# Conditioning of a two-block transformer kernel in 48 groups of one 2 MB load instead of 24 of two, spread evenly over the first mixer

## What is computed

```python
def ada_params(cvec, w, b):
    return jnp.split(jax.nn.silu(cvec) @ w + b, 6, axis=-1)   # w: 1024 x 6144
```

## Time and profile before

| what | value |
|---|---|
| median of three executions | 3366.84 us |
| the profiled execution's own time | 3363.03 us |
| its span, first to last instruction | 3361.3 us |
| mean granted TensorE clock | 0.903 |
| TensorE busy | 2707.1 us, 81% of the span |
| VectorE, ScalarE, GpSimd busy | 884.3, 402.9, 165.1 us |
| moved by the DMA engines | 721.65 MB, 215 GB/s in the mean |
| first mixer: first instruction to the last weighted sum | 0 to 625.9 us |

### The profile page before, as it was taken

How to read it: one execution, slowest core, us unless ns; L and a number is a source line. 1 busy time by engine, 2 the same in 40 slices (tenths; PEclk the granted TensorE clock), 3 DMA queues, 4 the chain that set the end, 5 groups by cost and what they waited for, 6 DMA issues and landing times.

```text
span 3361.3 us, 31421 instructions
## 1 busy us (share of the span) xinstructions
PE 2707.1 (81%) x12402; PEld 1478.8 (44%) x12402; DVE 884.3 (26%) x1870; ACT 402.9 (12%) x762; POOL 165.1 (5%) x199
## 2 busy tenths in 40 slices
PE   5877866579979987489979978888695768888887
PEld 2333433234434434344448544444383764444443
DVE  2143625520020011520023411111273564111111
ACT  1021311100010010210010100000113111000001
POOL 2001000010000002010000100000000001000000
PEclk8988987689989998789989999899797889989998
DMA  6446358434443443034454489999740005799997
GB/s 215 176 151 220 120 211 291 150 119 138 150 147 114 149 139 122 0 118 139 149 204 144 178 361 417 421 417 419 299 150 26 1 5 220 322 411 421 419 421 315
DMA packets 262667, 721.65 MB, mean 215 GB/s; under 512 B 13345, under 2 KB 146865, under 8 KB 208689
## 3 DMA queue, kind: packets, MB, share of 16 engines
q1 hardware_dynamic: 251232, 690.00, 54.1%
q0 software_dynamic: 11344, 30.40, 2.6%
HBM read 719.17 MB, written 1.18 MB: 214 GB/s over the span
## 4 chain that ended last, share of the span: by engine, by line
PE 65%; DMA 20%; DVE 9%; ACT 2%; SPq 2%; issue 2%; POOL 0%; DVEq 0%; ACTq 0%; POOLq 0%
PE ps L835 20%; DMA ring<-in_moe_w_up 13%; PE ps L1373 8%; PE ps L940 7%; DMA ring<-in_ada_w 5%; PE ps L860 5%; PE ps L1040 3%; PE ps L994 3%; PE ps L1022 3%; SPq L512 2%; PE ps L871 2%; PE ps L1363 2%; PE ps L840 1%; PE ps L1392 1%; PE ps L1313 1%
## 5 line engine op out<-in xcount | busy, mean ns | idle before, releaser
L835 PE MATMUL ps<-ring,hT 128*128 128x512 f32 x1600 | 711.9, 601 | 16.6 <-DMA ring<-in_ffn_w_in 5.1
L835 PEld LDWEIGHTS ps<-ring,hT 128*128 128x128 f32 x1600 | 305.6, 193 | 387.3 <-issue 374.6
L1373 PE MATMUL ps<-arena 128*32 128x512 f32 x1536 | 276.5, 700 | 76.9 <-DMA ring<-in_moe_w_up 66.9
L1373 PE MATMUL ps<-ring,arena 128*32 128x512 f32 x512 | 275.8, 701 | 0.0
L1363 PEld LDWEIGHTS ps<-arena,h 128*128 128x128 f32 x1024 | 248.4, 334 | 14.3 <-issue 10.7
L1363 PE MATMUL ps<-arena,h 128*128 128x128 f32 x1024 | 244.9, 398 | 2.5 <-issue 2.5
L940 PE MATMUL ps<-ring,arena 128*128 128x512 f32 x528 | 232.2, 592 | 2.3 <-ACT arena L1607 2.3
L994 PE MATMUL ps<-ring,cond 128*2 128x256 f32 (+1 forms) x1536 | 118.5, 476 | 139.1 <-DMA ring<-in_ada_w 136.4
L1982 DVE SCALAR_TENSOR_TENSOR arena<-ps,arena 128x256 f32<-128x256 f32 x66 | 28.0, 425 | 632.9 <-ACT arena L1603 632.9
L1373 PEld LDWEIGHTS ps<-arena 128*32 128x32 f32 x1536 | 67.2, 124 | 260.1 <-issue 186.7
L860 PE MATMUL ps<-hT,ring 128*128 128x256 f32 x768 | 170.9, 386 | 1.5 <-ACT hT L1536 1.5
(11 more groups left out here) (485 smaller groups left out, 2597.5 us busy)
## 6 DMA issues: line engine op xcount, KB each, us to landing
ring<-in_moe_w_down SPq DMA_DIRECT2D x128, 1024.0 KB, 17.4
ring<-in_ada_w SPq DMA_DIRECT2D x48, 2048.0 KB, 12.1
arena<-in_moe_w_gate SPq DMA_DIRECT2D x96, 1024.0 KB, 11.7
arena<-in_moe_w_up SPq DMA_DIRECT2D x96, 1024.0 KB, 9.8
ring<-in_ffn_w_in SPq DMA_DIRECT2D x66, 1024.0 KB, 8.6
ring<-in_ffn_w_out SPq DMA_DIRECT2D x33, 1024.0 KB, 5.0
ring<-in_moe_w_gate SPq DMA_DIRECT2D x32, 1024.0 KB, 15.5
ring<-in_moe_w_up SPq DMA_DIRECT2D x32, 1024.0 KB, 17.6
```

What stands on the lines that cost most here:

```text
L835: m = pe.matmul(o3, lhsT_of(k), ring[:, a:a + 2, k * EH:(k + 1) * EH], start=start and k == 0, stop=stop and k == KC - 1)
L1373: m = pe.matmul(ps[a * CAP:(a + 1) * CAP, 6, :].rearrange("p (u c) -> p u c", u=2), x_slots[:, k, a * CAP:(a + 1) * CAP], slot_pair(gate_s ...
```

## The change

The conditioning is cut into 48 groups of 512 columns. A group is one load of 2 MB (one pair of slots), four strips of 128 columns; its 32 products are half as wide. `group_rows` has four buffers of 128 columns (index g % 4 for g % 2 throughout), so the bias of group g+4 is loaded behind the store of group g, and all stores count on one semaphore. Four groups instead of two stand ahead of the first norm (banks 0, 1, 6 and 7), their rows are spread per group.

The ring is counted by pairs: `two_slots(hold=True)` takes a pair and marks it as held until `drop(s)`, and the count passes over held pairs. So a pair with weights of the mixer, which are used over several blocks, stays out of the rotation while groups pass through the other two pairs.

The order changes: one group behind every two blocks before the scan (7 in all), three groups in each scan step (24 in all: one behind the first block, ahead of the state products, and two behind the second; in step 7 behind the third), and 2, 2, 2, 2, 2, 1, 1, 1 in the mLSTM steps. The banks follow from the new `FILLS`. GpSimd's `post()` comes ahead of the store of group 8 (before: of group 3). Some semaphores are shared under new names (`exp_input` for two, `mod_stored` for two), with the same waits.

The core of the diff:

```diff
         self.pos = 0
+        self.held = set()
 
     def slots(self, n):
         at = [(self.pos + i) % SLOTS for i in range(n)]
         self.pos += n
         return at
 
-    def two_slots(self):
-        self.pos += self.pos % 2
-        return self.slots(2)
+    def two_slots(self, hold=False):
+        s = self.pos % SLOTS
+        while s in self.held:
+            s = (s + 2) % SLOTS
+        self.pos = s + 2
+        if hold:
+            self.held.add(s)
+        return s
+
+    def drop(self, s):
+        self.held.discard(s)
...
         ADA = [("ada_w", 0, (0, 1)), ("ada_w", 1, (2, 3)), ("ada_w_2", 0, (4,)), ("ada_w_2", 1, (5,))]
-        ADA_UNITS = 4
-        GROUPS_PER_LAYER = 6 * D // (ADA_UNITS * EH)
-        ADA_B = (1,) * 8
-        FIRST_GROUPS = 2
-        ADA_BEFORE_B = FIRST_GROUPS + 3 + 11
+        STRIPS, STRIP = 4, 128
+        GROUP = STRIPS * STRIP
+        GROUPS_PER_LAYER = 6 * D // GROUP
+        ADA_B = (2, 2, 2, 2, 2, 1, 1, 1)
+        FIRST_GROUPS = 4
+        ADA_BEFORE_B = FIRST_GROUPS + 7 + 24
         N_ADA = ADA_BEFORE_B + sum(ADA_B)
         assert N_ADA == GROUPS_PER_LAYER * len(ADA)
-        group_rows = junk[:, 0:2 * EH].rearrange("p (b c) -> p b c", b=2)
-
-
-        FILLS = [("v", t) for t in range(4)] + [("ada", 2)] + [("hg", j) for j in range(6)] + [("ada", 3)]
-        FILLS += [("gate", t) for t in range(4)] + [("ada", 4)]
+        group_rows = junk[:, 0:4 * STRIP].rearrange("p (b c) -> p b c", b=4)
+
+
+        FILLS = [("v", 0), ("v", 1), ("ada", 4), ("v", 2), ("v", 3), ("ada", 5)]
+        FILLS += [("hg", 0), ("hg", 1), ("ada", 6), ("hg", 2), ("hg", 3), ("ada", 7), ("hg", 4), ("hg", 5), ("ada", 8)]
+        FILLS += [("gate", 0), ("gate", 1), ("ada", 9), ("gate", 2), ("gate", 3), ("ada", 10)]
         FILLS_BEFORE_SCAN = len(FILLS)
-        FILLS += [("hg", 6), ("hg", 7), ("ada", 5), ("hg", 8), ("hg", 9), ("ada", 6), ("ada", 7), ("hg", 10), ("hg", 11), ("ada", 8)]
-        FILLS += [("rows", 0), ("rows", 1), ("ada", 9), ("ada", 10), ("qk", 0), ("qk", 1), ("ada", 11), ("qk", 2)]
-        FILLS += [("qk", 3), ("ml_v", 0), ("ada", 12), ("ml_v", 1), ("ml_v", 2), ("ml_v", 3), ("ada", 13), ("ada", 14), ("ml_gate", 0)]
-        FILLS += [("ml_gate", 1), ("ml_gate", 2), ("ml_gate", 3), ("ada", 15)]
-        STEP_GROUPS = ((5,), (6, 7), (8,), (9, 10), (11,), (12,), (13, 14), (15,))
+        STEP_BLOCKS = [(("hg", 6), ("hg", 7)), (("hg", 8), ("hg", 9)), (("hg", 10), ("hg", 11)), (("rows", 0), ("rows", 1)),
+                       (("qk", 0), ("qk", 1), ("qk", 2)), (("qk", 3), ("ml_v", 0), ("ml_v", 1)),
+                       (("ml_v", 2), ("ml_v", 3), ("ml_gate", 0)), (("ml_gate", 1), ("ml_gate", 2), ("ml_gate", 3))]
+        for i, blocks in enumerate(STEP_BLOCKS):
+            g = FIRST_GROUPS + 7 + 3 * i
+            early = 3 if i == 7 else 2
+            FILLS += [blocks[0], ("ada", g), *blocks[1:early], ("ada", g + 1), ("ada", g + 2), *blocks[early:]]
...
                 for _ in range(count):
                     name, j, _, _, _, col = ada_group_of(ada_next[0])
                     ada_next[0] += 1
-                    for u in range(2):
-                        s, s1 = n.two_slots()
-                        fill_two(s, I[name][j][:, col + 2 * EH * u:col + 2 * EH * (u + 1)])
-                        ada_free[s] = ada_free[s1] = ada_next[0]
-
-            def stream_two(src, blocks):
-
-                n.block += blocks
-                s, s1 = n.two_slots()
+                    s = n.two_slots()
+                    fill_two(s, I[name][j][:, col:col + GROUP])
+                    ada_free[s] = ada_free[s + 1] = ada_next[0]
+
+            def stream_two(src, last):
+
+                s = n.two_slots(hold=True)
                 fill_two(s, src)
-                free_at[s] = free_at[s1] = n.block
+                free_at[s] = free_at[s + 1] = BLOCK_NO[last]
+                return s
+
+            def stream_units(srcs, lasts):
+
+                s = n.two_slots(hold=True)
+                for u, (src, last) in enumerate(zip(srcs, lasts)):
+                    fill(s + u, src)
+                    free_at[s + u] = BLOCK_NO[last]
+                return s
...
             def unit(at):
-                stream([kmajor(w[:, at:at + EH])], 2)
-
-            stream_two(w[:, 512:1024], 4)
+                return kmajor(w[:, at:at + EH])
+
+            held = stream_two(w[:, 512:1024], ("v", 3))
             ada_groups(1)
-            for at in (0, 1536, 2048):
-                unit(at)
+            n.drop(held)
             ada_groups(1)
-            stream_two(w[:, 1024:1536], 4)
+            held = stream_units([unit(0), unit(1536)], [("hg", 1), ("hg", 3)])
             ada_groups(1)
-            unit(EH)
-            unit(1536 + EH)
+            n.drop(held)
+            ada_groups(1)
+            n.drop(stream_units([unit(2048)], [("hg", 5)]))
+            ada_groups(1)
+            held = stream_two(w[:, 1024:1536], ("gate", 3))
+            ada_groups(1)
+            n.drop(held)
+            ada_groups(1)
+            held = stream_units([unit(EH), unit(1536 + EH)], [("hg", 7), ("hg", 9)])
+            ada_groups(4)
+            n.drop(held)
+            ada_groups(2)
+            held = stream_units([unit(2048 + EH)], [("hg", 11)])
+            ada_groups(1)
+            n.drop(held)
+            ada_groups(5)
+            held = stream_two(w[:, 2560:3072], ("qk", 3))
             ada_groups(3)
-            unit(2048 + EH)
+            n.drop(held)
+            ada_groups(1)
+            held = stream_two(w[:, 3072:3584], ("ml_v", 3))
             ada_groups(3)
-            stream_two(w[:, 2560:3072], 4)
...
             def group_store(g):
 
                 _, _, _, m_, row, col = ada_group_of(g)
                 pool.wait_ge(sem("ada_rows_ready"), g + 1)
                 for r in range(m_):
-                    pool.dma_start(mod_dram[row + r, col:col + ADA_UNITS * EH].rearrange("(u n) -> u n", u=ADA_UNITS),
-                                   group_rows[r:r + 97:32, g % 2, :]).then_inc(sem(f"mod_stored_{g % 2}"), 16)
-                pool.wait_ge(sem(f"mod_stored_{g % 2}"), 16 * ada_stores_through(g))
-                if g + 2 < N_ADA:
-                    group_bias(g + 2)
+                    pool.dma_start(mod_dram[row + r, col:col + GROUP].rearrange("(u n) -> u n", u=STRIPS),
+                                   group_rows[r:r + 97:32, g % 4, :]).then_inc(sem("mod_stored"), 16)
+                pool.wait_ge(sem("mod_stored"), 16 * ada_stores_through(g))
+                if g + 4 < N_ADA:
+                    group_bias(g + 4)
 
             pool.wait_ge(sem("zero_ready"), 1)
-            group_bias(0)
-            group_bias(1)
+            for g in range(4):
+                group_bias(g)
             for i, src in enumerate((I["ctx"][0], I["x"][0])):
                 load(x_sb[:, 2 * i:2 * i + 2, :], src.rearrange("(t p) d -> p t d", p=P), x_loaded)
             load(v_tmp[:, :], row_all(I["norm_g"][0, 0]), sem("vectors_loaded"))
-            for g in range(2):
+            for g in range(4):
                 pool.wait_ge(sem("vectors_spread"), g + 1)
-                group_bias(g + 2)
+                group_bias(g + 4)
...
-            group_store(2)
             n.h += 4
             pool.wait_ge(h_ready, n.h)
-            post()
-            for g in range(3, ADA_BEFORE_B):
+            for g in range(4, ADA_BEFORE_B):
+                if g == 8:
+                    post()
                 group_store(g)
...
                     ada_next[0] += 1
-                    twos = [n.two_slots()[0] for _ in range(2)]
-                    for s in twos:
-                        filled(s)
-                    half = slice(EH * (g % 2), EH * (g % 2) + EH)
+                    s = n.two_slots()
+                    filled(s)
+                    part = slice(STRIP * (g % 2), STRIP * (g % 2) + STRIP)
                     for k in range(KC):
-                        for u in range(ADA_UNITS):
-                            m = pe.matmul(ps[32 * u:32 * u + m_, bank, half], cond[:, lo:lo + m_, k],
-                                          slot_two(twos[u // 2])[:, k, EH * (u % 2):EH * (u % 2 + 1)],
+                        for u in range(STRIPS):
+                            m = pe.matmul(ps[32 * u:32 * u + m_, bank, part], cond[:, lo:lo + m_, k],
+                                          slot_two(s)[:, k, STRIP * u:STRIP * (u + 1)],
                                           start=k == 0, stop=k == KC - 1, skip_group_check=True)
...
-            ada_groups(1, 0)
-            ada_groups(1, 1)
+            for g in range(2):
+                ada_groups(1, FIRST_BANK[g])
             pe.wait_ge(constants_loaded, 48)
-            for g in range(2):
+            for g in range(4):
+                if g < 2:
+                    ada_groups(1, FIRST_BANK[g + 2])
+                v, half = divmod(g, 2)
                 pe.wait_ge(sem("ada_rows_ready"), g + 1)
```

(51 more changed lines are left out.)

75 lines of the change are left out of this document (42 added, 33 removed).

## The result

The changed kernel takes **3318.0 us** in the median of 4 runs (3312.3 to 3326.7), beside 3365.1 for the kernel before: ratio 0.9864, 95% interval 0.984 to 0.9888. A second set gave 3322.1, ratio 0.9878 (0.9854 to 0.9902). The forecast was 3320. The total is near and the parts are not: the stage up to the last weighted sum gave 37 us where the sum had 51, and some of the rest came from behind the stage.

The account below looks back on a forecast made before the run. TensorE bounds the kernel, its waits for conditioning weights being the target. Terms 8 + 1 + 17 + 25 = 51 us off 3363.0, of which 47 were kept, give a median of about 3320 us; range 3300 to 3356.

Parts of the forecast that it names:

- after 625.8: Behind the first mixer's last weighted sum: last stores and output weights have over 30 us of cover, everything runs as before.
- the last term: The mLSTM steps' minus 25 us, trusted least of the terms; for it 47 of the summed 51 us were kept.
- A group's price: TensorE time of one halved conditioning group: 1.9 us behind steady work, 3.4 us at the lower clock.
- the rival of the kept length: Halved groups still take 3.6 us, as a record costs 57 ns whatever its columns; 3364 us, chance 0.08.
- the one with weight loads: Strips bound by twice as many TensorE weight loads, 6.1 us a group; plus 88 us, 3455 us, chance 0.05.
- Start and way to the scan: First transpose earlier by 8 us as the fourth load lands sooner; minus 1 us from there up to the scan.
- The scan: Eight scan steps, 317.6 us before: shorter groups and fewer load waits against new bank waits give 300.5, minus 17 us.
- All five late groups: Scan groups 15, 16, 19, 31, 34 wait for loads because the block just ahead frees their pair: 9.2, 2.1, 7.3, 7.3, 7.3 us.
- the second gate block: In scan step 3 it waits 9.7 us for VectorE to read the first gate block from the same bank.
- In steps 5 to 7 the readers are done earlier; 0: Late scan steps: no new wait of TensorE for a bank still being read, 0 us.
- The mLSTM steps: Eight steps after the scan: 15.2 us each falls to 12.3 on average, bound by VectorE instead of loads; minus 25 us.
- that rival: Lower clock throughout the mLSTM steps: sums take 4.6 us for 2.5, 14.2 a step; plus 15, 3335 us, chance 0.10.

Follow-up runs that it names:

- run 7: Changed kernel with each GpSimd store of conditioning rows and each bias load cut into two transfers of half the columns; 3327.2 us, ratio 0.9897.
- Run 3: Changed kernel with VectorE reading the first gate block of scan step 3 before the state updates instead of behind them; 3310.1 us, ratio 0.9834.
- run 4: Changed kernel with the ring handing out the free pair released longest ago instead of the next in turn; 3255.6 us, ratio 0.9675.
- Runs 2: Changed kernel with three or seven added TensorE products of no use behind the groups of each mLSTM step; 3312.5 us, ratio 0.9839.
- run 8: Changed kernel plus oldest released pair, early gate block read, two groups in each mLSTM step and three added products in each; 3233.1 us, ratio 0.9611.
- run 1: Changed kernel with the halved groups back in the old places, in bunches of two to four behind a step's early blocks; 3344.0 us, ratio 0.9939.
- run 9: Changed kernel with halved groups bunched in the old places and the ring handing out the pair released longest ago; 3320.2 us, ratio 0.9863.

## Why the prediction was right, and where it was not

**The total** was right: 47 forecast, 45.8 and 41 by the two ratios. Of this the stage gives 37 in each pair of profiles, and what lies behind it some 5 (2734.4 on average before, 2729.4 over eleven profiles made from the changed kernel). The forecast had the stage at 51 and "after 625.8" at nothing. Both were off: the stage gave 14 us less than its sum, which is more than a quarter, and that the total still fell on 3318 is in part luck. The 4 us held back for the last term covered some of the 14, and time behind the stage some more, which no term had.

**A group's price** was right: 1.93 us for 1.9, 3.60 for 3.4 at the lower clock. The overhead of some 60 cycles that the Trainium skill (TensorEngine Tiling, Instruction Overhead) gives each matmul does not show as a fixed part here: a record of 128 columns takes 30 ns, all in all, where one of 256 took 57. With it fall the rival of the kept length and the one with weight loads.

**Start and way to the scan** were right: 8.6 for 8, 0.9 for 1. But the forecast had the fourth load, group 3's, end last, near 33, and group 3 waited for nothing: it started at 34.97 behind the first spread records. What set the start was group 2's load (4.28 us of waiting, to 29.33) and, close behind it (run 7: 5.9 us later there gave 5.4), the mean squares of x, which the sum didn't name.

**The scan** was mis-sized: minus 8 (9 in the second pair of profiles), not 17. All five late groups were named and came within 1.5 us of their price (9.8, 3.2, 8.0, 8.7, 8.4 for 9.2, 2.1, 7.3, 7.3, 7.3), the second gate block to the decimal (9.73). The missing 9.2 us are three small terms: waits 59.3 for 55.3, among them 2.3 for qk2's reader, which the step "In steps 5 to 7 the readers are done earlier; 0" denied; groups 54.6 for 52.6, as each of the five late ones took 1.67 more and not 1.4 (7 in sum), and the others 1.93; and 195.8 for 192.6 of other work. The last is an omission: the forecast priced the lower level in the late group itself, but not in what follows a wait. The output products took 31.5 us for 29.2 before and the two gate blocks 15.7 for 14.1. Run 3 shows that 8.9 us less of stall gave 10.3, run 4 that 44.5 us less gave 57.

**The mLSTM steps** gave 19.8 us in one profile, 18 in the other, not 25. The step that failed is "I take 12.3 in the average for clock"; from sums to sums a step took 12.8 us in the first profile and 13.0 in the second. Steps with a sum at 2.5 us took 11.3, as reckoned; but the sums took 2.50 us in two steps only, and 31.4 for 20 in sum. The argument against that rival, "the sums follow a group directly, which warms the engine", is what failed: the sums follow VectorE's weights, and one group of 1.93 us followed by 4 to 5.6 of idle time left them at 4.67, a granted clock of 0.50. Two groups followed by 2.4 us left them at 2.50 in one step and at 3.94 in another. Runs 2 and 8 show that the clock is nearly all of it: with the sums at 2.50 throughout run 8 takes 92.7 us, and 104.1 less the 11.4 is as much. The rival named this at 0.10, with 2.1 us in each of eight sums; two thirds of it happened.

**GpSimd** did not bind (run 7). Its cycle was shorter than the forecast's 7.2 us: 5.1 to 7.3, 6.2 in the mean from 516 to 553 us, where it works without a pause. It begins to bind, by 4.8 us of VectorE's waits, when all eight steps have two groups and take 11.3 us (run 8).

**Freed early enough?** The forecast followed each pair and then took the late ones as the price of the change. Their cause, that the ring hands out pairs in turn and so often the one just released, was in those very lines. By it a rule that costs nothing was worth more than the change: 62 us against 46.

## What to carry to other kernels

When a ring of buffers serves users that hold them for different times, let it hand out the buffer released longest ago, in the loader's and in the user's count alike; and follow each late load back to who freed its buffer before accepting it. Price a stall of TensorE with the slower records behind it: here a microsecond of waiting cost 1.2 to 1.3. Halving a unit of work and spreading it are two changes: halving alone gave 21 us (run 1), spreading the halved groups 22 to 26 more, and 65 where buffers come free early (run 9). Spreading groups that are not halved was not tried.
